# The step sizes of a state-space layer leave the weight stream of a fused kernel: 32 columns in full precision, in four column groups

## What is computed

```python
h = rmsnorm(x, pre_norm[0])
z, xbc, dt = split(h @ w_in, [2048, 2048 + 4096])    # 2048 + 4096 + 32 columns
xbc = silu(causal_depthwise_conv(xbc, conv_w, conv_b))  # x, B, C
dt = softplus(dt + dt_bias)                          # step sizes, 32 heads
A = -exp(a_log)
a_cs = cumsum(dt * A) within chunks of 128 tokens
y = ssd_chunked(xs, dt, A, B, C) + d_skip * xs       # 8 groups of 4 heads
y = rmsnorm(y * silu(z), gate_norm)
x = x + rmsnorm(y @ w_out, post_norm[0])
```

## Time and profile before

| | |
|---|---|
| median of 3 runs | 1857.53 us (1856.58 to 1859.53) |
| span of the profiled execution, first to last instruction | 1854.7 us |
| TensorE busy | 1832.7 us, 99% |
| VectorE busy | 1073.5 us, 58% |
| GpSimd busy | 894.9 us, 48% |
| ScalarE busy | 548.6 us, 30% |
| mean granted clock of TensorE | 0.998 |

### The profile page before, as it was taken

The page is one execution under the profiler, slowest core; times in us unless marked ns, Lnnn a source line. Parts: engine busy times, 40 slices in busy tenths (PEclk is TensorE's granted clock), DMA queues, the critical chain, the costliest instruction groups (busy, mean ns, idle before and its releaser), DMA issues.

```text
span 1854.7 us, 25072 instructions
## 1 busy us (share of the span) xinstructions
PE 1832.7 (99%) x9700; PEld 1467.7 (79%) x9700; DVE 1073.5 (58%) x1673; ACT 548.6 (30%) x1014; POOL 894.9 (48%) x900
## 2 busy tenths in 40 slices
PE   9999999999999999999999999999999999999998
PEld 7888888788777777588888888877777788888887
DVE  7888888985887667553333312457888633333212
ACT  4544455513344330331111000235544211111001
POOL 6444444554533445255555556553433555555553
PEclk9999999999999999999999999999999999999999
DMA  9777677676754569488888888875653788888875
GB/s 243 171 149 159 147 155 163 148 168 142 174 115 102 130 161 238 119 189 186 197 192 189 195 185 201 197 170 129 134 126 75 167 191 191 195 194 192 186 167 135
DMA packets 216975, 309.11 MB, mean 167 GB/s; under 512 B 22750, under 2 KB 171418, under 8 KB 216858
## 3 DMA queue, kind: packets, MB, share of 16 engines
q0 software_dynamic: 42624, 147.87, 46.4%
q1 hardware_dynamic: 170970, 155.93, 27.2%
q10 hardware_dynamic: 3264, 3.71, 0.7%
HBM read 153.12 MB, written 2.10 MB: 84 GB/s over the span
## 4 chain that ended last, share of the span: by engine, by line
PE 92%; DVE 5%; DMA 1%; ACT 1%; issue 1%; POOL 0%; SPq 0%; DVEq 0%; POOLq 0%; ACTq 0%
PE gp L785 24%; PE gp L787 23%; PE gp L786 23%; PE gp L757 2%; PE gp L725 2%; PE gp L732 2%; PE gp L726 2%; PE gp L759 2%; PE gp L758 2%; PE mp L1198 1%; PE mp L1095 1%; PE mp L960 1%; PE mp L1059 1%; DMA wl<-stage 1%; DVE m_yl L2119 1%
## 5 line engine op out<-in xcount | busy, mean ns | idle before, releaser
L667 POOL TENSOR_SCALAR wh<-stage 128x1024 fp32r<-128x1024 f32 (+2 forms) x298 | 345.8, 1160 | 835.1 <-PE gp L787 677.5
L785 PE MATMUL gp<-hh,wh 128*128 128x512 f32 x1504 | 601.7, 400 | 1.7 <-DMA wl<-stage 1.3
L786 PE MATMUL gp<-hh,wl 128*128 128x512 f32 x1504 | 586.4, 390 | 0.0
L787 PE MATMUL gp<-hl,wh 128*128 128x512 f32 x1472 | 574.6, 390 | 0.0
L673 POOL TENSOR_SCALAR wl<-stage 128x1024 fp32r<-128x1024 f32 (+3 forms) x296 | 352.0, 1189 | 0.0
L785 PEld LDWEIGHTS gp<-hh,wh 128*128 128x128 f32 x1504 | 282.8, 188 | 72.4 <-issue 16.2
L786 PEld LDWEIGHTS gp<-hh,wl 128*128 128x128 f32 x1504 | 283.0, 188 | 56.9 <-issue 1.4
L787 PEld LDWEIGHTS gp<-hl,wh 128*128 128x128 f32 x1472 | 276.6, 188 | 59.4
L676 POOL DMA_DIRECT2D wl<-stage x296 | 262.9, 888 | 94.1 <-POOL wl L673 85.2
L2498 DVE TENSOR_TENSOR val<-gp,rstd 128x512 f32<-128x512 f32 x44 | 30.4, 692 | 205.5 <-PE gp L787 205.5
L2367 DVE TENSOR_TENSOR xT<-gp,xT 128x512 f32<-128x512 f32 x31 | 21.4, 689 | 194.7 <-PE gp L787 189.8
(11 more groups left out here) (387 smaller groups left out, 2758.5 us busy)
## 6 DMA issues: line engine op xcount, KB each, us to landing
wl<-stage POOLq DMA_DIRECT2D x262, 512.0 KB, 5.3
stage<-ffn_w SPq DMA_DIRECT2D x120, 512.0 KB, 4.4
stage<-ssm_w_in SPq DMA_DIRECT2D x32, 512.0 KB, 4.9
stage<-hg_w_in SPq DMA_DIRECT2D x32, 512.0 KB, 4.4
stage<-ssm_w_in SPq DMA_DIRECT2D x32, 256.0 KB, 5.0
stage<-ssm_w_out SPq DMA_DIRECT2D x16, 512.0 KB, 4.0
stage<-att_w_in SPq DMA_DIRECT2D x14, 512.0 KB, 4.5
stage<-cp_w_in SPq DMA_DIRECT2D x12, 512.0 KB, 5.9
```

Of the source, the lines that this page charges most:

```text
L667: pool.tensor_scalar(wh[:, s, part], stage[:, s, part], 1.0, 1.0, ALU.mult, ALU.mult).then_inc(hi_done, 1)
L785: pe.matmul(bank[:, :], wvh[:, cols], hi(kk), start=start, stop=False)
L786: pe.matmul(bank[:, :], wvl[:, cols], hi(kk), start=False, stop=False)
L787: mm = pe.matmul(bank[:, :], wvh[:, cols], lo(kk), start=False, stop=stop)
```

## The change

The 32 step-size columns are loaded apart, in full precision, into `dtw` (one DMA on SP's queue behind the last part of x). GpSimd multiplies them by the norm weights, ahead of the fifth half. After the sum of squares TensorE multiplies them with the unrounded x: slice k goes to column group k mod 4, 32 rows of the PSUM bank each, so that four partial sums arise (`group_dt`, 8 products). VectorE multiplies all of them by `rstd` in one instruction, and four products with `pick`, an identity repeated four times, fold the partial sums and set the four chunks into their layout (`fold_dt`, inside slot 2, between the halves of tile B). ScalarE reads the result from PSUM.

The first unit becomes the first z tile of group 0, and the unit at the end of group 0 shrinks to its second z tile; slot 4 of group 0 runs no tile. So the layer has 48 tiles instead of 49, in the same number of units. The parameter copies move to ScalarE ahead of its wait for the folded sums, VectorE takes the z tile first, and the clearing of `sqsum` is replaced by a copy in the first gated sum.

```diff
@@ plan
-    add("ssm", w["ssm_in"], [(0, SDT0, 32), (32, SDT0 - 96, 96)], whole)
+    add("ssm", w["ssm_in"], [(0, 0, P)], whole)
     for g in range(SG):
         add("ssm", w["ssm_in"], [(0, SI + g * UC, UC)], whole)
         add("ssm", w["ssm_in"], [(0, SB0 + g * P, P), (P, SC0 + g * P, P)], whole)
-        add("ssm", w["ssm_in"], [(0, g * UC, UC)], whole)
+        add("ssm", w["ssm_in"], [(0, g * UC, UC)] if g else [(0, P, P)], whole)
@@ build
+    def ssm_tile(g, j):
+
+        return phases["ssm"][2] + ((1, 2, 3, 4, 0, 5)[j] if g == 0 else 6 * g + j)
@@ SP
                 if q == HALVES:
                     load_x(3)
+                    sp.dma_start(dtw[:, :, :], ssm_w_in[0][:, SDT0:SDT0 + SH].rearrange("(k p) n -> p k n", p=P)
+                                 ).then_inc(dtw_landed, 16)
@@ GpSimd
+                if q == HALVES:
+                    pool.wait_ge(dtw_landed, 16)
+                    pool.wait_ge(prm_ready, 1)
+                    pool.tensor_tensor(dtw[:, :, :], dtw[:, :, :], prm[:, P_PRE:P_PRE + KT].unsqueeze(2).to_broadcast([P, KT, SH]),
+                                       ALU.mult).then_inc(dtw_scaled, 1)
                 pool.wait_ge(landed[s], count[s])
@@ TensorE
+                def group_dt():
+
+                    pe.wait_ge(dtw_scaled, 1)
+                    for k in range(0, KT, NCH):
+                        for b in range(NCH):
+                            mm = pe.matmul(mp[1][b * SH:(b + 1) * SH, :], dtw[:, k + b, :], xT[:, k + b, :],
+                                           start=k == 0, stop=k + NCH == KT)
+                    mm.then_inc(dt_grouped, 1)
+
+                def fold_dt():
+
+                    pe.wait_ge(pick_made, 1)
+                    pe.wait_ge(dt_scaled, 1)
+                    for c in range(NCH):
+                        mm = pe.matmul(mp[2][c * SH:(c + 1) * SH, 0:P], pick[:, :].bitcast(F32),
+                                       dt_sum[:, c * P:(c + 1) * P], start=True, stop=True)
+                    mm.then_inc(dt_folded, 1)
+
                 run(gran, 6)
                 sum_squares(pre_round[0])
+                group_dt()
...
-                        if g < SG and (g or slot > 1):
+                        if g == 0 and slot == 2:
+                            run(gran, 1)
+                            fold_dt()
+                            run(gran, 1)
+                        elif g < SG and (g or slot in (3, 5)):
                             run(gran, 1 if (g, slot) == (1, 1) else 2)
@@ ScalarE
-                tile_taken(act, 0)
-                act.activation(u[:, :], u[:, :], ACT.Identity, bias=hcol[:, 0:1]).then_inc(dt_read, 1)
+                act.wait_ge(prm_turned, 2)
+                step(act.activation(prm[:, 0:P], mp[0][:, 0:P], ACT.Copy))
+                act.activation(prm[:, 2 * P + 16:3 * P], mp[0][:, 2 * P + 16:3 * P], ACT.Copy).then_inc(prm_ready, 1)
+                act.wait_ge(dt_folded, 1)
+                act.activation(u[:, :], mp[2][:, 0:P], ACT.Identity, bias=hcol[:, 0:1]).then_inc(dt_read, 1)
@@ VectorE
-                tile_whole(dve, 0)
-                for c in range(NCH):
-                    cols = slice(c * P, (c + 1) * P)
-                    ins = dve.tensor_tensor(u[c * SH:(c + 1) * SH, :], gp[0][0:SH, cols], rstd[0:SH, cols], ALU.mult)
-                    if c < NCH - 1:
-                        step(ins)
-                ins.then_inc(bank_read[0], 1)
+                dve.wait_ge(dt_grouped, 1)
+                dve.tensor_tensor(dt_sum[:, :], mp[1][:, :], rstd[:, :], ALU.mult).then_inc(dt_scaled, 1)
+                take(0, 4)
                 take(0, 0)
                 take(0, 1)
-                dve.wait_ge(prm_turned, 2)
-                step(dve.tensor_copy(prm[:, 0:P], mp[0][:, 0:P]))
-                dve.tensor_copy(prm[:, 2 * P + 16:3 * P], mp[0][:, 2 * P + 16:3 * P]).then_inc(prm_ready, 1)
...
-                        if g < SG - 1 and slot >= 4:
+                        if g < SG - 1 and slot >= (4 if g else 5):
                             take(g, slot)
```

More of the change, by code:

```diff
@@ L218, in tiles_of @@
         return range(phases[name][2], phases[name][3])
-    ssm0 = phases["ssm"][2] + 1
+    def ssm_tile(g, j):
+        return phases["ssm"][2] + ((1, 2, 3, 4, 0, 5)[j] if g == 0 else 6 * g + j)
     halves, place = [], {}
@@ L326, in build @@
         cbm = R.take("m_cbm", [P, NCH, P])
+        g_at = R.at
         G = R.take("m_G", [P, HPG, L])
@@ L333, in build @@
         pick = R.take("m_pick", [P, SH], F32R)
+        R = Region(g_at)
+        dtw = R.take("m_dtw", [P, KT, SH])
+        dt_sum = R.take("m_dt_sum", [P, L])
         R = Region(after_y - 12 * 2048)
@@ L432, in build @@
         acs_split, pick_made = sem("acs_split"), sem("pick_made")
+        dtw_landed, dtw_scaled = sem("dtw_landed"), sem("dtw_scaled")
+        dt_grouped, dt_scaled, dt_folded = sem("dt_grouped"), sem("dt_scaled"), sem("dt_folded")
         prm_ready, dt_read, tap_ready, zsilu_ready = (sem(s) for s in (
@@ L1459, in last_tap @@
                 def last_tap(g, j):
-                    t = ssm0 + 6 * g + j
+                    t = ssm_tile(g, j)
                     n = 4 * g + j
@@ L1476, in silu_z @@
                 def silu_z(g, j):
-                    tile_taken(act, ssm0 + 6 * g + 4 + j)
+                    tile_taken(act, ssm_tile(g, 4 + j))
                     act.activation(z_of(g, j), z_of(g, j), ACT.Silu).then_inc(zsilu_ready, 1)
@@ L1956, in mamba @@
                 step(dve.memset(raw[:, :, 0:TAPS - 1], 0.0))
-                step(dve.memset(sqsum[:, :], 0.0))
                 def take(g, j):
-                    t, n = ssm0 + 6 * g + j, 4 * g + j
+                    t, n = ssm_tile(g, j), 4 * g + j
                     tile_whole(dve, t)
@@ L2105, in gate_rest @@
                     dve.wait_ge(gsq_ready, n + 1)
-                    ins = dve.tensor_tensor(sqsum[:, :], sqsum[:, :], sq[:, t, :], ALU.add)
+                    if n:
+                        ins = dve.tensor_tensor(sqsum[:, :], sqsum[:, :], sq[:, t, :], ALU.add)
+                    else:
+                        ins = dve.tensor_copy(sqsum[:, :], sq[:, t, :])
                     if n < 15:
```

## The result

| | before | changed |
|---|---|---|
| median of 21 runs each | 1856.95 us (1854.25 to 1859.53) | 1859.96 us (1858.70 to 1862.67) |
| ratio, 95% interval | | 1.0017 (1.0011 to 1.0023) |
| span of the profiled execution | 1854.7 us | 1859.3 us |
| TensorE busy | 1832.7 us | 1832.4 us |
| mean granted clock | 0.998 | 0.994 |

The changed kernel is 3.0 us slower by the medians and 4.6 us by the profiled spans; the forecast was +4.3 and 1861.8 us. A tile of 24 matmuls is gone (5.5 us), and yet TensorE's busy time is the same. The new products take 1.85 us and half a microsecond of it, and the products behind the idle gap run at half speed for 4.5 us, which takes about 2 us more. The rest goes with stretches of low clock later in this execution: changed_again, the same program with one of them less, has 1830.4 us busy.

A forecast was written before the change was run, and what follows sets the result against it. TensorE, busy 99% of the span, bounds the kernel. Chain +2.3 us (start's 0.5 taken off) and clock +2.0 sum to +4.3: span 1859.0, plus 2.8 to the median, 1861.8 us; forecast range 1859.5 to 1864.5, overall 1855.2 to 1864.5.

The forecast's parts named there:

- The 2.8 us added to the span: Whole kernel: the excess of the 1857.5 us median over the span, added to the forecast span 1859.0 to give 1861.8.
- Start: First unit's load, one DMA instead of two on SP's queue: everything 0.5 us earlier, bounds 0 and 0.9.
- group_dt: TensorE after the sum of squares: 8 added products, 16 records of 32 columns in four column groups, 1.8 us.
- rival 3: TensorE's thin products: column groups don't overlap, about 7 us in place of 1.8, later steps move by 5: 1867; chance 0.04.
- fold_dt: TensorE between the halves of tile B: 4 added products, 8 records of 128 columns, 0.4 us, between 0.3 and 0.66.
- The chain: Step sizes on ScalarE and VectorE, held up by GpSimd's four back-to-back halves: transposes +2.8 us, +2.3 after the start (1.5 to 3.5).
- The page's rule against the row: VectorE beside GpSimd: skill's lock for one instruction gives 1856.5; the row of L2010, waiting through two conversions (2.87 us), gives 1861.8.
- Rival 1: VectorE gets in after each single conversion: L895 at 51.4, idle 2.8 us without a clock fall, 1856.5; chance 0.22.
- The clock: TensorE behind the 6 us idle gap before the transposes: clock falls to half, 2.0 us lost (0 to 3.3).
- nothing takes the loss back: Behind L895: VectorE waits 2.04 us for a TensorE tile at 65.96, so TensorE sets the order to the end.
- the weights as the next limit: Group 1's first tile, chain hardly stalled: weights land at 52.6 against 52.0 needed, gain 3.2 us, 1854.3; chance 0.08.

The follow-up runs named there:

- changed_again: The changed kernel, unedited, measured a second time on one chip beside others: 1860.94 us, ratio 1.0020 to the kernel before.
- late_chain: Kernel before, with three waited-for copies on ScalarE ahead of the read of the step sizes, GpSimd's gap kept: 1856.66 us, ratio 1.0001.
- hold_gpsimd: Changed kernel, with GpSimd's third of four back-to-back halves waiting until the step-size tables are done: 1854.89 us, ratio 0.9990.
- z_early_only: Changed kernel, with group 0's second z tile moved ahead of B and C, fold still between the halves of tile B: 1854.77 us, ratio 0.9988.
- fold_first: Changed kernel, with the four folding products ahead of tile B instead of between its halves: 1854.55 us, ratio 0.9988.
- keep_clock: Changed kernel, with 24 unread products on constants ahead of the table transposes: 1859.07 us, ratio 1.0013; repeated 1859.14 us, ratio 1.0009.
- z_early: Changed kernel, with the second z tile of group 0 ahead of B and C and the folding products ahead of tile B: 1855.79 us, ratio 0.9993.
- fold_first_hold: Changed kernel, with the fold ahead of tile B and GpSimd's third half held until the step-size chain is through: 1854.67 us, ratio 0.9988.

## Why the prediction was right

**The time.** 1859.96 us against 1861.8 forecast, inside the range but near its lower end. Of the 1.8 us between them 0.6 is the base (1857.53 was a median of 3 runs, 1856.95 is one of 21) and 1.3 the difference of the medians, 3.0 us for 4.3. The 2.8 us added to the span were not all time around the kernel: in every profiled execution of the experiments the measured time is 1.8 to 1.9 us above the span, and the rest was that the profiled execution of before was a quick one. The position of C*B moved by 4.23 and 3.96 us, and the medians of the second measurement by 4.2.

**TensorE's part.** Start: 0.5 us forecast, 0.61 measured (8.99 against 9.60), of which up to 0.4 can be chance by the 9.20 of late_chain. group_dt: 1.8 us forecast for 16 records, 1.85 measured from its start to the next product; four column groups of 32 do overlap, rival 3 is out. With its changed neighbours the next tile starts 2.02 us later at that place (31.66 - 30.25 + 0.61). fold_dt: 0.4 forecast, 0.55 with the slower first products behind it (from 34.52, where the half tile ends, to 34.97, plus 0.1 that the first product there takes above the usual 0.23). Net, TensorE reached the transposes at 48.93; by the forecast (49.1 less 0.5) it was 48.6.

**The chain.** ScalarE read the folded sums at 35.10; 35.4 less the start's 0.5 was forecast, 34.9. The first convolution step began at 38.43, 38.25 forecast. GpSimd's four DMA issues stood at 43.28, 46.57, 49.85 and 53.13; 43.4, 46.7, 50.0 and, one row further than was written out, the end of the last conversion 53.0 were forecast with the start taken off, and that end came at 52.83. VectorE's stalled rows were the forecast ones: L2046 (L2014 before) waited through two conversions for 2.79 us, and of the convolution step at 47.34 the first took 2.77 us and the second 3.24. L929 at 54.42, 54.7 forecast. Idle 5.34 us, some 6 forecast. That this chain of cause is right and not only its sum was shown from three sides: take GpSimd's run apart by a wait (hold_gpsimd) or by another order (z_early_only), and the chain ends at 49.7 and 49.3; start the chain late with the gap in place (late_chain), and nothing is lost; start it early with the run in place (fold_first), and most of it is through before the run begins.

**The page's rule against the row.** The prediction set the Trainium skill, "SBUF — State Buffer", section "Who interferes with whom", by which the first to issue holds the pair for one instruction, against a row with two conversions. Rows of the changed kernel side with the row: 2.79, 2.77 and 3.24 us for instructions that take 0.3 to 0.8 us alone, each through two conversions. All three started while GpSimd's row of a DMA issue ran (43.56, 47.34 and 50.14, with issues from 43.28, 46.57 and 49.85 of 0.9 us each); the one at 47.34 started 0.17 us behind the start of the conversion's row, so it isn't only the 0.6 us ahead of that row that count. Rival 1, at 1856.5, took one conversion per instruction and would have had L895 at 51.4.

**The clock.** 2.0 us forecast between 0 and 3.3; 1.9 and 1.5 shown by keep_clock and by its repetition. This was the term without a row of its own, and here the fall did come behind idleness alone (near 52.1, with nothing on TensorE since 49), as the Trainium skill's "TensorE: Matmul & The Clock Gate", section "Part 1: The HAM clock gate", has it. My estimate took the length of a low stretch from the earlier trace rows, 3.3 us, and the stretch here was 6.8 us long (52.1 to 59.0). As 2.3 us of that lay in the idle gap and 4.5 behind it at half speed, 2.3 us at most could be lost, and the term held for a reason that I had not worked out: that much was luck.

**What was behind it.** The prediction said that nothing takes the loss back and that TensorE sets the order to the end; the table of positions bears out the first. It named the weights as the next limit behind a chain that is not stalled, at 3.2 us of gain (3.3 + 0.5 - 0.6). fold_first found that wait, 0.74 us, and moved its transposes by 3.0 us (52.36 to 49.34), where 3.8 was the sum. Of the 0.8 between them 0.4 are group_dt and the fold as measured above and 0.54 is the wait for the scaled sums at 32.30; 0.2 came back at the start (0.73 earlier than before, not 0.5). Less the wait for the weights that leaves 2.3 us; C*B moved by 2.0 and the median by 1.9. The last 0.3 us is how a wait reads: idle time counts from the end of the last product's row, 0.16 us behind the point where the next would have followed, and the first product behind the gap takes 0.31 us instead of 0.23.

**What was not foreseen.** That the loss could be undone by moving one call ahead of half a tile. The prediction saw that the chain's start lay 1.3 us later and walked VectorE's list from there, but didn't ask what another start would give; the start decided which of VectorE's instructions came to stand in GpSimd's run, and 2.2 us of start were worth 6.7 us at the end.

## What to carry to other kernels

Before matmuls are taken out ahead of a join, follow the engine that prepares weights: its work is triggered by TensorE's progress, and an earlier TensorE can close the gaps in which another engine, held up by that work, was getting its own done. Start the small chain that a join waits for ahead of that run, or put a pause into the run; here either was worth some 6 us at C*B, more than the tile that was saved. A wait at a join costs more than its length where the clock falls in it (5.3 us of idleness, 1.5 to 1.9 us on top), and moving other work ahead of the wait doesn't help while the queue behind it is late as a whole. When effects of 1 us are to be read, compare positions in the profiles from the same first step on; the medians here spread by more than that.

## What the runs showed of the hardware

- **Back-to-back work of GpSimd starves VectorE.** With the next conversion 0.6 us behind a DMA issue, a run of halves repeats every 3.3 us, and in each turn one of VectorE's instructions can be held through both conversions (2.79, 2.77, 3.24 us); the short ones behind it still fit in (L2047 and L2049 at 46.27 and 46.52). In the 14 profiles, between 30 and 70 us, 32 instructions of VectorE waited through two conversions, and each had started while GpSimd's row of a DMA issue ran; those held through one (0.96 to 1.57 us) had all started otherwise. The reverse doesn't hold: in z_early a convolution instruction started at 50.51, inside such a row (49.76, 0.89 us), and ran at once, and the conversion came later. What decides is open. Where GpSimd had started from idleness, none waited through more than one conversion (0.96 us for L2042 at 42.11, which takes 0.29 at 39.09 in fold_first, with GpSimd idle). In hold_gpsimd the three instructions of the convolution step took 2.32 us with no conversion beside them.
- **The clock's low stretches differ in length, and later ones come and go.** 3.3 us in the earlier trace rows, 6.8 us here. Apart from the end of the span, windows of 20 us with a clock under 0.95 stood at 40 to 60, 660 to 680 and 1400 to 1420 in the changed kernel, at 40 to 60 and 660 to 680 in changed_again, which is the same program. The window from 1400, first in the changed kernel, then in changed_again:

```profile
1400.00:1420.00 20.00, 17.74 (x146) 13.87 (x145) 15.08 (x39) 7.63 (x15) 4.05 (x4) 0.83 0.37 81
```

```profile
1400.00:1420.00 20.00, 17.33 (x163) 13.35 (x162) 17.46 (x43) 9.36 (x17) 4.05 (x4) 1.00 0.37 81
```

  The span of changed_again is 1856.7 us against 1859.3, though its C*B stands only 0.27 us earlier. The mean granted clock is on record for the executions without a profile too, and the time goes with it: of the 101 executions of the kernel before beside the experiments, the 17 with a clock of 0.998 have a median of 1854.85 us, the 53 with 0.997 one of 1856.47, the 27 with 0.996 one of 1857.98 and the 4 with 0.995 one of 1859.12. So such falls go with most of the spread among runs of one kernel. One execution of fold_first_hold (0.945, 1859.44 us) lies far off this line and was not followed.
- **Thin products in four column groups.** 16 records of 32 columns in full precision over 512 tokens took 1.85 us, 0.12 each, where the two records of the sum of squares, over all columns, take 0.96 (28.66 to 29.62).
